# Pairs of squares and the last scan's low parts moved from GpSimd to VectorE, two steps of the gate and one of up reordered

## The reference, cut to what matters

```python
def rms_norm(x, gain):
    xf = x.astype(jnp.float32)
    y = xf * lax.rsqrt(jnp.mean(xf * xf, axis=-1, keepdims=True) + NORM_EPS)
    return (y * gain.astype(jnp.float32)).astype(x.dtype)
...
        mix = jnp.concatenate([rms_norm(attn, attn_out_g[i]), rms_norm(mlp, mlp_out_g[i])], axis=-1) @ w_o[i]
        h = h + rms_norm(mix, post_mix_g[i])
        f = conv_ffn(rms_norm(h, pre_ffn_g[i]), w_up[i], conv_w[i], conv_b[i], w_down[i])
        h = h + rms_norm(f, post_ffn_g[i])
        gate = jax.nn.sigmoid(rms_norm(h, ple_norm_g[i]) @ w_ple_gate[i])
        h = h + gate * (p[i] @ w_ple_proj[i])
```

## Time and profile before

| | us |
|---|---|
| median of 3 runs (lowest, highest) | 2454.4 (2454.36, 2455.34) |
| profiled execution | 2455.45 |
| span of its core, first to last instruction | 2453.6 |
| TensorE busy, 15278 matmuls | 2270.5 (93%) |
| VectorE busy | 1468.0 (60%) |
| ScalarE busy | 1089.7 (44%) |
| GpSimd busy | 274.9 (11%) |
| L3018, GpSimd's adds of squares, 36 of them | 56.3, mean 1564 ns |
| mean granted TensorE clock, share of full speed | 0.975 |

### The profile page before, as it was taken

The page is one execution under the profiler, slowest core; times in us unless marked ns, Lnnn a source line. Parts: engine busy times, 40 slices in busy tenths (PEclk is TensorE's granted clock), DMA queues, the critical chain, the costliest instruction groups (busy, mean ns, idle before and its releaser), DMA issues. The chain is left out here.

```text
span 2453.6 us, 36142 instructions
## 1 busy us (share of the span) xinstructions
PE 2270.5 (93%) x15278; PEld 1872.6 (76%) x15278; DVE 1468.0 (60%) x2217; ACT 1089.7 (44%) x1735; POOL 274.9 (11%) x147
## 2 busy tenths in 40 slices
PE   7999889789999977898899999998998899999997
PEld 5888667578888866686588888886786688888876
DVE  2133573749778786557667666346467577666255
ACT  3211472557568573336634333244246534334243
POOL 0000101524123250101010000001101010000011
PEclk8999999899999988999999999999999999999999
DMA  9121106211112112230112223231320022222321
GB/s 367 52 69 52 35 2 226 100 46 59 53 44 61 53 53 92 86 138 18 46 70 87 94 95 103 98 117 52 118 107 18 18 69 93 97 103 88 110 103 52
DMA packets 35201, 205.19 MB, mean 84 GB/s; under 512 B 3936, under 2 KB 5472, under 8 KB 14816
## 3 DMA queue, kind: packets, MB, share of 16 engines
q1 hardware_dynamic: 35040, 202.88, 23.3%
HBM read 200.77 MB, written 2.10 MB: 83 GB/s over the span
## 5 line engine op out<-in xcount | busy, mean ns | idle before, releaser
L300 PE MATMUL ps<-a_high,w_high 128*128 128x512 f32 (+1 forms) x1680 | 627.4, 373 | 38.2 <-DVE a_low L2604 18.3
L301 PE MATMUL ps<-a_low,w_high 128*128 128x512 f32 (+1 forms) x1680 | 619.3, 369 | 0.0
L302 PE MATMUL ps<-a_high,w_low 128*128 128x512 f32 (+1 forms) x1680 | 619.0, 368 | 0.0
L300 PEld LDWEIGHTS ps<-a_high,w_high 128*128 128x128 f32 x1680 | 318.3, 189 | 102.0 <-issue 18.4
L2222 DVE TENSOR_TENSOR w_low<-raw_ring,w_high 128x2048 fp32r<-128x2048 f32 x102 | 234.7, 2301 | 263.0 <-ACT w_high L2216 258.3
L2216 ACT ACTIVATE w_high<-raw_ring 128x2048 fp32r<-128x2048 f32 x102 | 195.3, 1915 | 370.1 <-PE ps L302 282.4
L301 PEld LDWEIGHTS ps<-a_low,w_high 128*128 128x128 f32 x1680 | 318.4, 190 | 53.5 <-issue 1.4
L302 PEld LDWEIGHTS ps<-a_high,w_low 128*128 128x128 f32 x1680 | 318.3, 189 | 52.7
L300 PE MATMUL ps<-x_high,place_high 128*128 128x512 f32 (+1 forms) x704 | 250.8, 356 | 15.1 <-POOL place_low L292 7.8
L301 PE MATMUL ps<-x_low,place_high 128*128 128x512 f32 (+1 forms) x704 | 245.3, 348 | 0.0
L302 PE MATMUL ps<-x_high,place_low 128*128 128x512 f32 (+1 forms) x704 | 244.9, 348 | 0.0
(11 more groups left out here) (395 smaller groups left out, 4040.7 us busy)
## 6 DMA issues: line engine op xcount, KB each, us to landing
raw_ring<-w_dram SPq DMA_DIRECT2D x110, 1024.0 KB, 4.9
arena<-w_dram SPq DMA_DIRECT2D x26, 1024.0 KB, 7.7
place_raw<-wc_dram SPq DMA_DIRECT2D x48, 512.0 KB, 3.6
place_raw<-w_dram SPq DMA_DIRECT2D x11, 1024.0 KB, 4.9
ab_raw<-w_dram SPq DMA_DIRECT2D x10, 1024.0 KB, 5.0
x<-xT_dram SPq DMA_DIRECT2D x4, 512.0 KB, 13.8
out_dram<-x SPq DMA_DIRECT2D x1, 2048.0 KB, 7.2
arena<-r_dram SPq DMA_DIRECT2D x2, 992.0 KB, 5.9
```

The lines of the kernel that those rows point to most:

```text
L300: nc.tensor.matmul(out, wh, xh, start=start, stop=False)
L301: nc.tensor.matmul(out, wh, xl, start=False, stop=False)
L302: return nc.tensor.matmul(out, wl, xh, start=False, stop=stop)
```

## The change

1. The low parts of `yh` 0 to 6 go to VectorE (`y_low`): 0 to 3 between `keys` and `states` of the last head, 4 and 5 after `gate` and ahead of the first `masks`, 6 after the second `masks`. That of 7 stays where it was.
2. GpSimd's block in the tail goes; the same adds are made by VectorE (`pair`, `next_pairs`): two of each projection ahead of the second `meet` or `join`, one in the first half at k = 4, and the six over the new X behind the second half (for the gate three ahead of the low part of u_g+1 and three behind it). Each waits for the one before (`S.pooled`).
3. In `up`, TensorE's sums of up0 move behind the first half tile of unit 1, those of up1 behind unit 1.
4. In the gate, ScalarE splits u_g+1 ahead of `next_squares(1)` and not behind; VectorE makes the low part of u_g+2 ahead of the inverse of "ple" and not behind unit 0's scaling; TensorE's sums of "ple" move from behind unit 0 into unit 1, between its half tiles.

```diff
@@ stage_c, gpsimd
-                    for k in range(KT - 1):
-                        pool.wait_ge(S.rms_high, k + 1)
-                        nc.gpsimd.tensor_tensor(xl[k][:, 0:L], yh[:, k, :], xh[k][:, 0:L].bitcast(f32), O.subtract)\
-                            .then_inc(S.operand, 1)
@@ stage_c, vector
+                    def y_low(k, done):
+                        dve.wait_ge(S.rms_high, k + 1)
+                        nc.vector.tensor_tensor(xl[k][:, 0:L], yh[:, k, :], xh[k][:, 0:L].bitcast(f32), O.subtract)\
+                            .then_inc(done, 1)
...
                             keys(h)
+                            if h == CH - 1:
+                                for k in range(4):
+                                    y_low(k, S.operand)
                             states(h)
                             weigh(h)
                         if t >= 2:
                             gate(t - 2)
+                        if h == CH - 1:
+                            y_low(4, S.operand)
+                            y_low(5, S.operand)
                         for dr in range(2):
                             if 0 <= h < CH:
                                 masks(h, 2 * dr)
                                 masks(h, 2 * dr + 1)
+                                if h == CH - 1 and dr == 0:
+                                    y_low(6, S.operand)
@@ stage_tail, tensor, up
-                            if s == 1:
-                                sums("up0", halves[0], sq)
...
                                 if s == 1 and h == 0:
-                                    sums("up1", halves[1], sq)
+                                    sums("up0", halves[0], sq)
                             last.then_inc(S.pe_tile, 1)
+                        sums("up1", halves[1], sq)
@@ stage_tail, tensor, gate
                                 last = tile(u_g + m, h, PS[:, PAIR[m] + h, :], slice(0, L), range(KT))
+                                if m == 1 and h == 0:
+                                    sums("ple", slice(0, L), sq)
...
-                            if m == 0:
-                                sums("ple", slice(0, L), sq)
@@ stage_tail, scalar
+                        split(u_g + 1, "dn11B")
                         next_squares(1)
-                        split(u_g + 1, "dn11B")
@@ stage_tail, vector
+                        def pair(n, k, ts):
+                            dve.wait_ge(S.squares, n)
+                            if pairs[0]:
+                                dve.wait_ge(S.pooled, pairs[0])
+                            pairs[0] += 1
+                            nc.vector.tensor_tensor(sq[:, 0:2, ts], sq[:, 0:2, ts], sq[:, k:k + 2, ts], O.add)\
+                                .then_inc(S.pooled, 1)
...
                                     join(3, 1)
+                                    pair(11, 4, halves[1])
+                                if s == 0 and k == 4 and name == "wo":
+                                    pair(5, 4, halves[1])
...
                         meet("wo2A", 2, 0)
+                        pair(2, 2, slice(0, L))
+                        pair(3, 4, halves[0])
                         meet("wo3A", 3, 0)
                         half("wo", 0, u_up)
                         split_low(dve, u_up + 1)
                         half("wo", 1, None)
+                        next_pairs(0, 0)
+                        next_pairs(0, 1)
                         split_low(dve, u_up + 2)
...
                         join(2, 0)
+                        pair(8, 2, slice(0, L))
+                        pair(9, 4, halves[0])
                         join(3, 0)
                         half("dn", 0, u_g)
                         half("dn", 1, None)
+                        next_pairs(8, 0)
                         split_low(dve, u_g + 1)
+                        next_pairs(8, 1)
...
                             if m == 0:
+                                split_low(dve, u_g + 2)
                                 inverse("ple", 1, slice(0, L))
...
-                            if m < 3:
+                            if m in (1, 2):
                                 split_low(dve, u_g + m + 2)
```

More of the change, by code:

```diff
@@ L1677, in norms @@
                             nc.vector.tensor_tensor(x, x, ln_root[:, halves[s]], O.mult).then_inc(S.res_next, 1)
[L1679 to L1682, removed]
+                    y_low(KT - 1, S.kept)
                     out_low(OUT + 4)
@@ L3008, in _ @@
                             sp.wait_ge(S.load, loads)
[L3010 to L3038, removed]
                     @block.tensor
@@ L3397, in operand, with next_pairs @@
                                                            O.mult, O.subtract).then_inc(S.operand, 1)
+                        pairs = [0]
+                        def pair(n, k, ts):
[5 more added lines that the diff above has]
+                                .then_inc(S.pooled, 1)
+                        def next_pairs(n, s):
+                            for i in range(1, 4):
+                                dve.wait_ge(S.res_squares, n + 4 * s + i + 1)
+                                if pairs[0]:
+                                    dve.wait_ge(S.pooled, pairs[0])
+                                pairs[0] += 1
+                                nc.vector.tensor_tensor(sq[:, 0:2, halves[s]], sq[:, 0:2, halves[s]],
+                                                        sq[:, 2 * i:2 * i + 2, halves[s]], O.add).then_inc(S.pooled, 1)
                         def join(m, s):
```

## The result

The changed kernel takes 2442.38 us in the median of 6 runs (2439.49 to 2446.14), beside 2456.3 (2454.36 to 2460.78) for the kernel before in the same job: ratio 0.9948, 95% interval 0.9938 to 0.9958, 12.8 us less. In a second job the ratio was 0.9957 (0.9943 to 0.9971), 10.6 less. The forecast was 18.0 less.

What follows compares the result with a forecast made beforehand. TensorE, busy 93% of the span, was taken as the bound, with time only in its gaps, low clock or removable work. 5.0 + 1.6 + 11.4 = 18.0 us gave 2436.4 us; range 2432 to 2442.5.

Steps and rivals of the forecast that it cites:

- The centre: An add moved onto VectorE costs it less (0.6 us) than the same add beside it on GpSimd (1.1 us).
- rival 3: Everywhere adds move: the stretch is VectorE's own, not GpSimd's doing, so the kernel gets slower, 2460.6 us; chance 0.02.
- Part 1: Last scan, once: low parts moved to VectorE remove TensorE's 4.6 us gap and the low clock; 5.0 us gained.
- the bounds: Last scan: gain between 2.5 us (clock stays low in the gather steps) and 5.5 us.
- Part 2: Out-projection and `up`, twice: adds moved to VectorE and later sums gain 0.8 us each, 1.6 for both.
- rival 1: `up`, both layers: the clock falls in both new gaps ahead of tile 3, price 2 x 1.6 us, 2439.6; chance 0.25.
- a sign of being wrong: `up`: the forecast is wrong if the clock drops to 0.5 at either gap.
- Part 3: Down projection and gate, twice: unit 0 starts earlier and waits for sums go; 5.7 us each, 11.4 for both.
- rival 2: Down projection, second half: ScalarE bounds it, a gap and low clock stay, 2.7 us each, 2442.4; chance 0.12.
- the edge: Gate: unit 3's low part ends at 2426.2, just when wanted; 0.1 us taken for it.

Runs made afterwards that it cites:

- pairs_only: The kernel before with the pairs of squares on VectorE and all else as before, last scan too; ratio 0.9971, 7.1 us less.
- scan_only: The kernel before with point 1 of the change alone (low parts of yh 0 to 6 on VectorE); ratio 0.9992, 2.0 us less.
- gate_back: The changed kernel with point 4 of the change undone (the gate's old order); ratio to the kernel before 0.9984, 3.9 us less.
- sums_up_back: The changed kernel with point 3 of the change undone (old places of up0's and up1's sums); ratio to the kernel before 0.9932, 16.7 us less.

## Why the prediction was right and wrong

**The centre holds.** A GpSimd add that reads SBUF beside a two-input VectorE instruction costs VectorE more (0.9 to 1.1 us) than the same add made by VectorE (0.6, or 0.8 where each waits for the one before). Put back it stretches VectorE; a memset does not; rival 3 falls. Each row that was stretched beside a moved add is back at its short time; what is left of GpSimd's work in the scan still stretches a row (1.05 us at 891.94, for 0.41).

**Part 1, 5.0 forecast, 7.4 in this execution.** The chain went as written: products at 907.97 with no wait, clock 1.00 behind them. Of the extra 2.4 us, 2.2 were not mine to claim. GpSimd's L1452 waited for VectorE (7.44 us, above), where before it had stretched a `keys` row (2.58 us at 893.54). In both traces it starts 0.02 to 0.03 us behind the start of a VectorE instruction; why the order came out differently is not shown. Over all traces the scan takes 48.9, 48.5 and 44.9 us with the old code (`pairs_only` is the third) and 40.7 to 45.1, mean 43.0, in the eleven with the new: 4.4 less in the mean. By the medians `scan_only` gave 2.0, at most 4.4. So 5.0 was rather too much, and the bounds should have let this interleaving in, to both sides.

**Part 2, 0.8 each forecast, -0.9 and -2.5: here is the step that failed.** All of the working up to the gap came true: tile 3 starts 7.0 us earlier after 6.2 at the out-projection (0.8), and its gap is 2.78 (about 3.0). Then the prediction says that "3.0 lies nearest to the stretch that kept its clock, and I take that". It did not keep it: a low clock followed the gap of 2.76 to 2.78 us in all 12 passages of the six traces that have it, at some 1.6 us each, as rival 1 priced it; the prediction itself had named this as a sign of being wrong. The row chosen for comparison (533.90) is one draw, of a gap of 2.97 us. In two of 14 traces the clock fell behind this same gap; here in `gate_back`:

```profile
538.16 0.50 PE L300 MATMUL ps<-x_high,place_high 128*128 128x512 f32 x1 [2.97 <-POOL place_low L292]
```

```profile
538.40:542.20 3.80, 3.80 (x13) 2.97 (x13) 0.00 (x0) 3.80 (x4) 2.06 (x1) 0.67 0.66 164
```

The trace of before also had a row against the choice, which the prediction does not mention. At the end of the last scan TensorE stands idle for 0.96 us, works for 0.66, and stands idle for 2.29 us; behind that the matmuls come 0.43 us apart:

```profile
934.93 0.79 PE L300 MATMUL ps<-x_high 128*128 128x512 f32 x1 [2.29 <-DVE x_low L1681]
...
935.94 0.63 PE L302 MATMUL ps<-x_high,x_low 128*128 128x512 f32 x1
936.37 0.63 PE L300 MATMUL ps<-x_high 128*128 128x512 f32 x1
```

The clock was low behind this gap in 12 of the 14 traces. So length alone does not decide: the longest of the three nearly always keeps the clock, and the shorter one ahead of tile 3 never did. What makes the difference is not shown. The advice of the Trainium skill ("TensorE: Matmul & The Clock Gate", section "Why this matters for your kernels") to leave no idle gaps between bursts of matmuls is meant for gaps longer than the 2.78 us measured here; the clock fell all the same, and the measurement decides. A second miss lies in the same place. The prediction saw that the sums come one half tile later and that the chain behind them does not become shorter, and took this as a gain that does not arrive. `sums_up_back` shows it as a loss, 1.3 us of chain and 1.6 of clock each: without that step there is neither the longer chain nor the wide gap.

**Part 3, 5.7 each forecast, 4.9 and 5.2.** Unit 0 starts 0.29 us after the projection, so ScalarE is no bound and rival 2 falls. Unit 1 and the sums begin at 2394.78; before, they began at 2408.24 in a trace that was 7.8 us behind at the projection: 5.7 us earlier, where 5.8 was counted, and no wait is left ahead of the sums. Of that 0.5 is given back by the end of the span. Part of it is unit 3, whose first matmul (2418.73) starts some 0.47 us after the last of unit 2 and not 0.23, since its low part ends just too late, the edge that the prediction named (it took 0.1 there). I have traced the rest to no row. `gate_back` shows that most of the gain hangs on the new order (7.2 of the 10.2 us that both layers gain here in the traces).

**Elsewhere, 0 forecast, -1.2, and 1.6 of layer 1's `up`.** At 1994.82 there is a gap of 1.47 us which the kernel before has too. Here a low clock followed; before it did not. Of 28 such passages in the 14 traces, 6 lost the clock. Such places are a source of the spread of single executions, up to 10 us between the lowest and the highest run of one kernel in a job, and the range of the prediction (2432.0 to 2442.5) had nothing for them: one median lies just inside it (2442.38), the other outside (2445.02).

In sum: 18.0 less 3.2 for the clock behind the two gaps is 14.8; the two jobs gave 12.8 and 10.6. The rest of 2 to 4 us goes with the scan (0.6 by the mean of the traces, 3.0 by the medians of `scan_only`), with part 3 (1.2), with the clock behind the 1.47 us gap, which both traces of the changed kernel show in layer 1 and the trace of before does not (1.6), and with places that no single trace can settle. How often the clock falls there with the new code and how often with the old stays open; it would take many profiles of each.

## What to carry to other kernels

Ahead of giving GpSimd an elementwise job beside a busy VectorE, compare VectorE's neighbouring rows with and without it: here each 128x512 add beside a VectorE instruction with two SBUF inputs cost VectorE 0.9 to 1.1 us, and would have cost it 0.6 to 0.8 to do itself. When a removed stall lets TensorE run ahead, look at what it waits for next, and count the clock behind the new gap as lost unless several traces show it kept; one row is one draw. A wait of 1.3 us that leads early into a long chain can be worth more than the dense order that removes it.

## What the runs showed of the hardware that was not expected

- The clock behind an idle gap of TensorE is no function of the gap's length: 2.76 to 2.78 us ahead of tile 3 lost it 12 times in 12, 2.97 us at 534 lost it 2 times in 14, 2.29 us at the end of the last scan (behind 0.96 idle and 0.66 of work) 12 times in 14, 1.47 us in the out-projection 6 times in 28.
- Ten matmuls of ones (2.4 us of TensorE work) in a gap whose length they don't change were worth 1.6 us each time.
- The same code of the last scan takes 40.7 to 45.1 us, or 44.9 to 48.9 with the old code, and whether VectorE or GpSimd waited at one instruction (7.44 or 2.62 us for the same GpSimd subtraction) is part of it.
